# Running the first weight tiles behind each norm on unnormalised rows, in a two-layer hybrid encoder on one NeuronCore

## Chip, core and metric

The kernel runs on one of the NeuronCores of a Trainium2 chip. The metric is the device time of one execution in microseconds. Its time is 1211.0 us, the median of three runs (1208.95 to 1211.0).

## What is computed

Two layers run over 288 tokens (256 of a prompt, 32 of a later chunk), held with features on the partitions, so that one token is one column. Of the reference only this matters here:

```python
def rms_norm(x, g):
    xf = x.astype(jnp.float32)
    y = xf * lax.rsqrt(jnp.mean(xf * xf, axis=-1, keepdims=True) + EPS)
    return (y * g.astype(jnp.float32)).astype(x.dtype)
...
    h = rms_norm(x, g1) * (1 + scale1) + shift1
    y, rows = token_mixers(h, w_in, f_bias, lnv_g, lnv_b, w_s, b_s, w_branch, w_gate, b_gate, w_out, past)
    x = x + gate1 * y
    h = rms_norm(x, g2) * (1 + scale2) + shift2
    f, conv_state = conv_ffn(h, w_up, w_conv, b_conv, w_down, conv_prefix)
    x = x + gate2 * f
```

Scale, shift and gate come from c (adaLN), one set for the prompt and one for the later chunk. The root of a norm is one number per token. So a product W h equals the product of W with the unnormalised rows (x g (1 + scale)), times that number for each column, plus W shift. A last RMSNorm follows the second layer.

## The kernel before, in words

Every weight matrix is cut into pieces of 128 x 1024 floats, each the weights of one output tile of 128 features, or a third of one in the down projection. 142 pieces of a layer go through a ring of four slots. SP loads a piece into `raw`; ACT rounds it to the high part `whi` (L1052, L1059); POOL subtracts, which gives the low part `wlo` (L512); PE multiplies. ACT works three pieces ahead of PE (`AHEAD`). Rows are split the same way into `hh` and `hl`. PE forms high x high, high x low and low x high (L603, L604, L605), so a full tile of eight k steps takes 24 matmuls of 288 or 290 columns. The semaphores `hi_ready`, `lo_ready` and `piece_done` count pieces.

The order on each engine is written out by hand. A layer runs 26 input tiles, 32 gate and 8 branch pieces between which the four mixers are placed, 8 output tiles, 44 up tiles (with a convolution of width 3 on VectorE and ScalarE) and 24 down pieces. Around a norm all of it is serial. DVE adds each finished output or down tile into `x` (L1747, L1814). ACT squares it (L1070). `sums` on PE adds the eight squares over the partitions with a matrix of ones, eight fp32 matmuls at L574, all after the last tile. ACT takes logarithm and exponential (L1074, L1075). Three Newton steps on DVE follow (L1364 to L1366). Then for each of eight k DVE multiplies `x` by the root (L1428) and applies scale and shift (L1433), ACT makes `hh` (L1082), POOL makes `hl` (L530), and PE's first tile takes the k steps as they come.

At the start PE works on the modulation of layer 0 (quads, L556) while its 8 MB of weights arrive. The sums of `x` stand before the seventh quad. DVE takes the quads' rows (L1371), PE turns them (L565), DVE adds the bias (L1378) and forms the scale (L1385, L1386), and only then does the norm. In the first mixer tiles PE swaps rows for the rotary (`swap`, L646) and DVE rotates (L1446 to L1448).

In these rows `ps` is PSUM (8 banks). Input and output tiles alternate between banks 0 and 1, up tiles between 0 and 3, the sums are in bank 7.

## Time and profile before

| | |
|---|---|
| Median of 3 runs | 1211.0 us |
| The profiled execution: its time, its span | 1210.8 us, 1209.0 us |
| PE busy | 1138.7 us (94%), 8368 matmul records |
| PEld, DVE, ACT, POOL busy | 1028.3, 491.3, 572.6, 703.4 us |
| HBM traffic | 178 GB/s over the span |
| Share of the chain that ended last | PE 88%, DVE 7% |

### The profile page before, as it was taken

To read this page: it belongs to the slowest core of one execution; us is meant where nothing else is said; L and a number is where in the kernel's file an instruction comes from. 1 tells how busy PE (TensorE), PEld (TensorE's weight loads), DVE (VectorE), ACT (ScalarE), POOL (GpSimd) and SP (SyncE) were. 2 spreads that over 40 slices of the span, in tenths; PEclk is the share of its full clock that TensorE was granted. 3 is DMA by queue.
4 is the path that set the end of the run, shared out by engine and by line. 5 is a ranking of instruction groups with operands and counts; after the bars stand their busy time and mean duration, and the time that the engine had idled before them with its cause. 6 is when DMAs were issued, how large, how long until landed. Compare 5 with 4: busy or idle time off the path is not lost.

```text
span 1209.0 us, 22886 instructions
## 1 busy us (share of the span) xinstructions
PE 1138.7 (94%) x8368; PEld 1028.3 (85%) x8368; DVE 491.3 (41%) x1141; ACT 572.6 (47%) x1014; POOL 703.4 (58%) x320
## 2 busy tenths in 40 slices
PE   5699999999999899999969999999999979999997
PEld 1497888888889799999958788888889969999996
DVE  0535523446223644441043482345641354544202
ACT  1354444445444456554324635455544446556432
POOL 0664534545456677778846544344556657777882
PEclk9699999999999799999988999999999979999999
DMA  9655536755554244445554564575534414544551
GB/s 362 240 177 217 217 141 239 257 223 196 197 187 140 71 173 163 152 170 174 177 182 144 174 232 184 210 272 173 163 117 126 153 67 162 173 150 162 175 180 71
DMA packets 61814, 215.90 MB, mean 179 GB/s; under 512 B 7896, under 2 KB 8480, under 8 KB 61488
## 3 DMA queue, kind: packets, MB, share of 16 engines
q1 hardware_dynamic: 61744, 214.92, 51.0%
q8 instruction: 49, 0.80, 0.3%
q14 instruction: 21, 0.17, 0.0%
HBM read 209.85 MB, written 5.05 MB: 178 GB/s over the span
## 4 chain that ended last, share of the span: by engine, by line
PE 88%; DVE 7%; ACT 1%; DMA 1%; issue 1%; SPq 1%; POOL 0%; DVEq 0%; ACTq 0%
PE ps L603 25%; PE ps L604 24%; PE ps L605 24%; PE ps L556 4%; PE ps L574 1%; DVE work L1428 1%; DMA first<-mod_first 1%; DVE hup L1433 1%; PE ps L550 1%; DVE work L1433 1%; DVE ps L1573 1%; PE ps L770 1%; DVE merged L1581 1%; PE ps L736 1%; PE ps L646 1%
## 5 line engine op out<-in xcount | busy, mean ns | idle before, releaser
L512 POOL TENSOR_TENSOR wlo<-raw,whi 128x1024 fp32r<-128x1024 f32 x284 | 678.6, 2392 | 450.6 <-ACT whi L1052 383.7
L603 PE MATMUL ps<-hh,whi 128*128 128x288 f32 (+1 forms) x1760 | 541.9, 308 | 39.4 <-POOL hl L530 37.6
L604 PE MATMUL ps<-hl,whi 128*128 128x288 f32 (+1 forms) x1760 | 528.0, 300 | 0.0
L605 PE MATMUL ps<-hh,wlo 128*128 128x288 f32 (+1 forms) x1760 | 527.3, 300 | 0.0
L603 PEld LDWEIGHTS ps<-hh,whi 128*128 128x128 f32 x1760 | 337.6, 192 | 86.6 <-issue 65.4
L604 PEld LDWEIGHTS ps<-hl,whi 128*128 128x128 f32 x1760 | 339.7, 193 | 0.2
L605 PEld LDWEIGHTS ps<-hh,wlo 128*128 128x128 f32 x1760 | 338.3, 192 | 0.0
L1052 ACT ACTIVATE whi<-raw 128x1024 fp32r<-128x1024 f32 x204 | 214.3, 1053 | 125.8 <-PE ps L605 112.9
L1306 ACT ACTIVATE conv<-ps,vec 128x290 f32<-128x290 f32 x88 | 52.3, 595 | 114.7 <-DVE ps L1768 114.4
L604 PE MATMUL ps<-fal,whi 128*128 128x290 f32 x352 | 104.5, 297 | 0.0
L603 PE MATMUL ps<-fah,whi 128*128 128x290 f32 x352 | 104.3, 296 | 0.0
L605 PE MATMUL ps<-fah,wlo 128*128 128x290 f32 x352 | 104.2, 296 | 0.0
L1097 ACT ACTIVATE gb<-ps,vec 128x288 f32<-128x288 f32 x64 | 32.1, 502 | 118.0 <-PE ps L605 118.0
L1059 ACT ACTIVATE whi<-raw 128x1024 fp32r<-128x1024 f32 x80 | 85.1, 1064 | 0.0
L1088 ACT ACTIVATE proj<-ps,cst 128x288 f32<-128x288 f32 x52 | 26.1, 502 | 115.0 <-PE ps L605 114.9
L1770 DVE SCALAR_TENSOR_TENSOR conv<-ps,vec,conv 128x290 f32<-128x290 f32 x88 | 45.8, 520 | 84.4 <-ACT tail L1310 84.4
L604 PEld LDWEIGHTS ps<-fal,whi 128*128 128x128 f32 x352 | 66.8, 190 | 0.0
L605 PEld LDWEIGHTS ps<-fah,wlo 128*128 128x128 f32 x352 | 66.6, 189 | 0.0
L603 PEld LDWEIGHTS ps<-fah,whi 128*128 128x128 f32 x352 | 66.4, 189 | 0.0
L1814 DVE SCALAR_TENSOR_TENSOR x<-ps,mod,x 128x256 f32 (+1 forms) x32 | 10.3, 363 | 124.6 <-PE ps L605 124.6
L1771 DVE SCALAR_TENSOR_TENSOR conv<-ps,vec,conv 128x290 f32<-128x290 f32 x88 | 45.8, 520 | 11.9 <-DVE conv L1770 0.5
L603 PE MATMUL ps<-oh,whi 128*128 128x288 f32 x128 | 40.8, 319 | 6.8 <-DVE hl L1559 3.6
(216 smaller groups left out, 1138.1 us busy)
## 6 DMA issues: line engine op xcount, KB each, us to landing
raw<-stream SPq DMA_DIRECT2D x284, 512.0 KB, 4.3
mraw<-stream SPq DMA_DIRECT2D x40, 1024.0 KB
first<-mod_first SPq DMA_DIRECT2D x16, 512.0 KB, 10.7
o_proj<-proj SPq DMA_DIRECT2D x12, 288.0 KB
kvk<-keys_t SPq DMA_DIRECT2D x6, 512.0 KB, 3.8
kvv<-vals SPq DMA_DIRECT2D x6, 512.0 KB, 4.7
cst<-consts SPq DMA_DIRECT2D x1, 1238.0 KB, 17.5
x<-x_fm SPq DMA_DIRECT2D x1, 1152.0 KB, 11.7
```

What stands on the lines that cost most here:

```text
L512: nc.gpsimd.tensor_tensor(wlo[:, slot, :], raw[:, slot, :], whi[:, slot, :].bitcast(F32), ALU.subtract).then_inc(lo_ready, 1)
L556: i = mm(ps[32 * g:32 * g + 32, bank, :], cpad[:, at + 30 - 2 * j:at + 62 - 2 * j], pieces[g // 2][:, (g % 2) * 512:(g % 2 + 1) * 512], st ...
L603: mm(out, whi[:, slot, a:b], high, start=(i == 0 and wcols[2]), stop=False)
L604: mm(out, whi[:, slot, a:b], low, start=False, stop=False)
L605: last = mm(out, wlo[:, slot, a:b], high, start=False, stop=(i == n - 1 and wcols[3]))
L1052: A(whi[:, slot, :], raw[:, slot, :], ACT.Copy).then_inc(hi_ready, 1)
L1059: A(whi[:, slot, :], raw[:, slot, :], ACT.Copy).then_inc(hi_ready, 1)
L1088: A(proj[:, t, :], ps[:, bank, 0:T], ACT.Copy, scale=cst[:, C_QS + t:C_QS + t + 1]).then_inc(bank_free[bank], 1)
L1097: A(gb[:, g % GB, :], ps[:, t % 2, 0:T], ACT.Sigmoid if g in DIRECT else ACT.Identity, bias=vec[:, v:v + 1]).then_inc(bank_free[t % 2], 1)
L1306: A(conv[:, u, :], ps[:, UPB + u, 2:2 + CC], ACT.Identity, scale=vec[:, at(V_CONV + 2 * 2 * FT + g * FT)], bias=vec[:, at(V_CB + g * FT)])
L1770: conv_link(V.scalar_tensor_tensor(conv[:, u, :], up[:, 1:1 + CC], w[1], conv[:, u, :], ALU.mult, ALU.add))
L1771: V.scalar_tensor_tensor(conv[:, u, :], up[:, 0:CC], w[0], conv[:, u, :], ALU.mult, ALU.add).then_inc(convolved, 1)
```

## The change

At the first norm of layer 1 the first six input tiles (`NI`), and at the second norm of each layer the first four up tiles (`NU`), take unnormalised rows.

- While output or down tiles run, DVE adds a tile back in its PSUM bank (`add_back`). ACT squares it there and makes its scaled high part `oh`, DVE the low part `ol`. Then DVE copies it to `x` and frees the bank. Two extra columns of `oh` and `ol` carry the shift, so its product comes out in two extra columns of the tile.
- PE takes the sum of a tile's squares after the next tile (`sum_square`), the last one in the middle of the first unnormalised tile (`first_tile`).
- DVE multiplies a finished unnormalised tile by the root per column (`scale_tile`), ACT adds the shift's product (`take_scaled`, `shift_up`). In between, for the tiles behind, the rows are normalised in chunks (`normed`, `IN_CHUNKS`, `UP_CHUNKS`). The root stands in PSUM bank 7 and the product x * root in PSUM too. POOL takes lows of rows and of weights in order of arrival.
- The first three pieces of layer 1 are loaded and split before layer 0 ends.
- At the start the sums stand before the sixth quad. DVE takes root and x * root before the modulation and makes the weight lows of pieces 0 and 1. PE runs input tiles 0 and 1 together, k step by k step, and DVE makes `hl`, which POOL made before.
- SWAP_BANK, the turning of w and its spreading move by a bank or a tile. The loops over output and down tiles are written out.

The core of the diff:

```diff
+IN_CHUNKS = ((0, 1), (1, 3), (3, 5), (5, 7), (7, 8), (8, 8))
+UP_CHUNKS = ((0, 2), (2, 5), (5, 8))
...
+NI, NU = 6, 4
...
+                if l == 0:
+                    pool.wait_ge(hl_ready, upto(l, hl_ready, KT))
+                    q = Q_IN + 2
+                else:
+                    q = lows_and_norm(Q_IN + AHEAD, 1, ((3, 0, 1), (1, 1, 4), (1, 4, KT)))
+                lows(q, Q_UP + AHEAD)
+                q = lows_and_norm(Q_UP + AHEAD, 2, ((1, 0, 2), (1, 2, 5), (1, 5, KT)))
+                lows(q, NSPLIT + (AHEAD if l + 1 < DEPTH else 0))
...
+                def first_tile(out, slot, n):
+
+                    product(out, slot, (1, 0, True, False), u_terms[0:4], ul_ready, (n - 2) * KT)
+                    sum_square(l, n, KT - 1)
+                    return product(out, slot, (1, 0, False, True), u_terms[4:KT], ul_ready, (n - 2) * KT + 4)
...
+                for m in range(KT):
+                    t = OUT_TILE + m
+                    tile_piece(slot_for(l, Q_OUT + m), Q_OUT + m, t % 2, t // 2, merged_l if m == 0 else None)
+                    if m:
+                        sum_square(l, 2, m - 1)
...
+                    up_piece(slot_for(l, Q_UP + j), Q_UP + 4 + j, UPB + j, j + 1 if j >= 2 else None, hl_ready if j == 0 else None)
...
+                    for g, ((a, b), c, o) in enumerate(zip(((0, TP), (TP, T)), cols, (0, TP + 2))):
+                        i = A(oh[:, m, o:o + b - a], ps[:, bank, c:c + b - a], ACT.Copy, scale=norm_a[:, n - 1, m, g:g + 1])
+                    i.then_inc(uh_ready, 1)
...
                         q = Q_UP + 2 * p + g + AHEAD
-                        if q < NSPLIT:
-                            high(q, q % RING)
+                        if q >= Q_UP + AHEAD + 3:
+                            high(q)
...
+            dve.wait_ge(rstd_guess, upto(0, rstd_guess, 1))
+            newton(first_link, DM)
+            for k in range(KT):
+                V.tensor_tensor(work[:, k, :], x[:, k, :], rstd[:], ALU.mult).then_inc(x_scaled, 1)
+            mod_take(0, MOD_A_PAIRS)
+            for q in range(2):
+                dve.wait_ge(hi_ready, upto(0, hi_ready, q + 1))
+                V.tensor_tensor(wlo[:, q, :], raw[:, q, :], whi[:, q, :].bitcast(F32), ALU.subtract).then_inc(lo_ready, 1)
...
+                def normed(n, a, b):
+
+                    half = [ps[:, bank, 2:2 + T] for bank in (6, 2 if n == 1 else 1)]
+                    at = (n - 1) * KT
+                    for k in range(a, b + 1):
+                        if k < b:
+                            if k > 1:
+                                dve.wait_ge(h_scaled, upto(l, h_scaled, at + k - 1))
+                            V.tensor_tensor(half[k % 2], x[:, k, :], ps[:, 7, 0:T], ALU.mult).then_inc(x_scaled, 1)
+                        if k > a:
+                            dve.wait_ge(x_scaled, upto(l, x_scaled, at + k))
+                            affine(n, k - 1, half[(k - 1) % 2])
...
+                def add_back(n, m, bank, gate_at, cols):
+
+                    parts = list(enumerate(zip(((0, TP), (TP, T)), cols, (0, TP + 2))))
+                    for g, ((a, b), c, o) in parts:
+                        y = ps[:, bank, c:c + b - a]
+                        i = V.scalar_tensor_tensor(y, y, mod[:, gate_at + m, g:g + 1], x[:, m, a:b], ALU.mult, ALU.add)
+                    i.then_inc(residual, 1)
+                    dve.wait_ge(uh_ready, upto(l, uh_ready, (2 - n) * KT + m + 1))
+                    if m == 0:
+                        V.tensor_tensor(ol[:, :, TP:TP + 2], mod[:, 24 * (n - 1):24 * (n - 1) + KT, :],
+                                        oh[:, :, TP:TP + 2].bitcast(F32), ALU.subtract)
+                    for g, ((a, b), c, o) in parts:
+                        i = V.scalar_tensor_tensor(ol[:, m, o:o + b - a], ps[:, bank, c:c + b - a], norm_a[:, n - 1, m, g:g + 1],
+                                                   oh[:, m, o:o + b - a].bitcast(F32), ALU.mult, ALU.subtract)
+                    i.then_inc(ul_ready, 1)
+                    for g, ((a, b), c, o) in parts:
+                        i = V.tensor_copy(x[:, m, a:b], ps[:, bank, c:c + b - a])
+                    i.then_inc(bank_free[bank], 1)
...
+                convolve(0, 0, 0)
+                scale_tile(Q_UP + 3, up_bank(3), 2, None)
+                convolve(0, 0, 1)
```

Three places show how instructions move. The first is ACT behind the second norm of layer 0, where `whi<-raw` rounds a weight piece, `hh` is the high part of a row tile and `conv` a tile of the convolution. Before:

```order
L1323 ACT_TABLE_LOAD
L1052 ACTIVATE whi<-raw 128x1024 [waits raw_loaded1,ol_ready,piece_done,tail_stored,proj_stored]
L1306 ACTIVATE conv<-ps,vec 128x290 [waits state_in]
L1310 ACTIVATE tail<-ps 128x4
L1052 ACTIVATE whi<-raw 128x1024 [waits piece_done,raw_loaded2]
L1306 ACTIVATE conv<-ps,vec 128x290 [waits state_in]
L1310 ACTIVATE tail<-ps 128x4
L1052 ACTIVATE whi<-raw 128x1024 [waits piece_done,raw_loaded3]
L1306 ACTIVATE conv<-ps,vec 128x290 [waits state_in]
L1310 ACTIVATE tail<-ps 128x4
L1316 ACTIVATE ps<-conv 128x290 [waits convolved]
L1052 ACTIVATE whi<-raw 128x1024 [waits piece_done,raw_loaded0]
```

Now, from the last three high parts on:

```order
L1156 ACTIVATE hh<-hup 128x290 [waits h_scaled] x3
L1423 ACTIVATE conv<-ps,vec 128x290 [waits ol_ready,state_in,tail_stored,proj_stored]
L1427 ACTIVATE tail<-ps 128x4
L1384 ACTIVATE ps<-ps,shifts 128x256 [waits up_scaled]
L1384 ACTIVATE ps<-ps,shifts 128x32
L1423 ACTIVATE conv<-ps,vec 128x290 [waits state_in]
L1427 ACTIVATE tail<-ps 128x4
L1423 ACTIVATE conv<-ps,vec 128x290 [waits state_in]
L1427 ACTIVATE tail<-ps 128x4
L1433 ACTIVATE ps<-conv 128x290 [waits convolved]
L1109 ACTIVATE whi<-raw 128x1024 [waits piece_done,raw_loaded0]
L1423 ACTIVATE conv<-ps,vec 128x290 [waits state_in]
```

Before, a piece was rounded ahead of every convolved tile; now the first one after the norm's three (into slot 0, the seventh up piece) stands behind three convolved tiles.

The second is POOL at the same norm. Before:

```order
L512 TENSOR_TENSOR wlo<-raw,whi 128x1024 [waits hi_ready]
L511 REGISTER_ALU
L512 TENSOR_TENSOR wlo<-raw,whi 128x1024 [waits hi_ready]
L519 REGISTER_ALU
L519 COMPARE_AND_BRANCH
L512 TENSOR_TENSOR wlo<-raw,whi 128x1024 [waits hi_ready] x2
L530 TENSOR_TENSOR hl<-hup,hh 128x290 [waits hh_ready] x8
L519 UNCONDITIONAL_BRANCH
```

Now:

```order
L542 REGISTER_ALU
L542 COMPARE_AND_BRANCH
L535 TENSOR_TENSOR wlo<-raw,whi 128x1024 [waits hi_ready] x4
L553 TENSOR_TENSOR hl<-hup,hh 128x290 [waits hh_ready] x2
L535 TENSOR_TENSOR wlo<-raw,whi 128x1024 [waits hi_ready]
L553 TENSOR_TENSOR hl<-hup,hh 128x290 [waits hh_ready] x3
L535 TENSOR_TENSOR wlo<-raw,whi 128x1024 [waits hi_ready]
L553 TENSOR_TENSOR hl<-hup,hh 128x290 [waits hh_ready] x3
```

The eight lows of rows stood together; now a weight low goes ahead of each chunk of two, three and three.

The third is DVE at the start, up to the first k steps. Before:

```order
L1371 COPY mod_rows<-ps 128x512 [waits mod_read,c_ready]
L1378 TENSOR_TENSOR mod<-ps,mvec 128x4x2 [waits rows_turned]
L1378 TENSOR_TENSOR mod<-ps,mvec 128x4x2 x3
L1385 TENSOR_SCALAR norm_a<-mod 128x16 [waits mod_ready]
L1386 TENSOR_TENSOR norm_a<-norm_a,mvec 128x16 [waits c_ready]
L1364 SCALAR_TENSOR_TENSOR rstd<-ps,rstd 128x288 [waits rstd_guess,c_ready]
L1365 SCALAR_TENSOR_TENSOR rstd<-rstd 128x288 [waits dve_own]
L1366 SCALAR_TENSOR_TENSOR rstd<-rstd 128x288 [waits dve_own]
L1428 TENSOR_TENSOR work<-x,rstd 128x288 [waits dve_own]
```

Now:

```order
L1490 SCALAR_TENSOR_TENSOR ps<-ps,rstd 128x288 [waits rstd_guess,c_ready]
L1491 SCALAR_TENSOR_TENSOR ps<-ps,rstd 128x288 [waits c_ready]
L1492 SCALAR_TENSOR_TENSOR rstd<-ps,rstd 128x288 [waits c_ready]
L1532 TENSOR_TENSOR work<-x,rstd 128x288 [waits c_ready]
L1532 TENSOR_TENSOR work<-x,rstd 128x288 x7
L1497 COPY mod_rows<-ps 128x512 [waits mod_read]
L1536 TENSOR_TENSOR wlo<-raw,whi 128x1024 [waits hi_ready] x2
L1504 TENSOR_TENSOR mod<-ps,mvec 128x4x2 [waits rows_turned]
L1504 TENSOR_TENSOR mod<-ps,mvec 128x4x2 x3
L1511 TENSOR_SCALAR norm_a<-mod 128x16 [waits mod_ready]
L1512 TENSOR_TENSOR norm_a<-norm_a,mvec 128x16 [waits c_ready]
L1554 TENSOR_SCALAR work<-work,norm_a,mod 128x256 [waits x_scaled,c_ready]
```

The root and the eight products of x moved ahead of the taking of the modulation's rows (`mod_rows`), and two weight lows (`wlo`) stand behind it.

## Rows read from the trace of the kernel before

**Rows 1.** Stretches; each pair: busy us (count) of PE, PEld, DVE, ACT, POOL; clock, DMA, GB/s

```profile
57.00:387.00 330.00, 326.04 (x2518) 281.08 (x2517) 140.16 (x311) 156.71 (x267) 171.47 (x73) 0.99 0.57 202
387.00:410.00 23.00, 15.87 (x65) 12.58 (x64) 13.63 (x34) 8.91 (x16) 10.17 (x11) 0.70 0.10 38
410.00:616.00 206.00, 206.00 (x1539) 206.00 (x1538) 72.77 (x187) 106.72 (x200) 152.69 (x64) 1.00 0.50 169
616.00:645.00 29.00, 15.81 (x64) 12.55 (x63) 18.20 (x29) 11.47 (x18) 17.04 (x13) 0.65 0.38 124
645.00:967.00 322.00, 316.55 (x2449) 277.92 (x2448) 136.56 (x304) 156.50 (x267) 172.46 (x73) 1.00 0.53 182
```

**Rows 2.** Waits of the whole span: engine, line, releaser, us in total, times, longest

```profile
PEld ps L603 <- issue: 69.0, 56, 12.2
...
PE ps L603 <- POOL hl L530: 37.6, 26, 11.8
```

**Rows 3.** Timeline of PE at the start: start us, us, engine, line, operation [idle before]

```profile
25.03 6.14 PE L574 MATMUL ps<-work,cst 128*128 128x288 f32 x16
31.10 1.92 PE L556 MATMUL ps<-first,cpad 128*32 128x512 f32 x16
...
43.93 0.58 PE L603 MATMUL ps<-hh,whi 128*128 128x288 f32 x1 [8.96 <-POOL hl L530]
```

**Rows 4.** Timeline of ACT at the start

```profile
32.15 2.93 ACT L1052 ACTIVATE whi<-raw 128x1024 fp32r<-128x1024 f32 x3
...
61.41 0.50 ACT L1088 ACTIVATE proj<-ps,cst 128x288 f32<-128x288 f32 x1 [1.76 <-PE ps L605]
```

**Rows 5.** Timeline of DVE at the start

```profile
33.16 0.69 DVE L1371 COPY mod_rows<-ps 128x512 f32<-128x512 f32 x1 [14.28 <-PE ps L556]
...
41.07 0.83 DVE L1428 TENSOR_TENSOR work<-x,rstd 128x288 f32<-128x288 f32 x2
41.81 0.62 DVE L1433 TENSOR_SCALAR work<-work,norm_a,mod 128x256 f32<-128x256 f32 x2
...
42.71 1.10 DVE L1433 TENSOR_SCALAR work<-work,norm_a,mod 128x256 f32<-128x256 f32 x2
```

**Rows 6.** Timeline of PE at the second norm of layer 0

```profile
387.48 4.05 PE L574 MATMUL ps<-work,cst 128*128 128x288 f32 x16
396.91 0.58 PE L603 MATMUL ps<-hh,whi 128*128 128x290 f32 x1 [5.38 <-POOL hl L530]
```

**Rows 7.** Timeline of DVE before, in and after the second norm of layer 0

```profile
371.69 0.65 DVE L1747 SCALAR_TENSOR_TENSOR x<-ps,mod,x 128x256 f32<-128x256 f32 x2 [2.54 <-PE ps L605]
...
387.69 0.64 DVE L1747 SCALAR_TENSOR_TENSOR x<-ps,mod,x 128x256 f32<-128x256 f32 x2 [2.57 <-PE ps L605]
...
392.57 0.46 DVE L1364 SCALAR_TENSOR_TENSOR rstd<-ps,rstd 128x288 f32<-128x288 f32 x1 [3.98 <-ACT rstd L1075]
...
426.98 0.16 DVE L1768 COPY ps<-vec 128x2 f32 x1 [0.43 <-PE ps L605]
428.12 0.52 DVE L1770 SCALAR_TENSOR_TENSOR conv<-ps,vec,conv 128x290 f32<-128x290 f32 x1 [0.98 <-ACT tail L1310]
```

**Rows 8.** Timeline of POOL beside it: a weight low and an activation low

```profile
369.70 2.40 POOL L512 TENSOR_TENSOR wlo<-raw,whi 128x1024 fp32r<-128x1024 f32 x1 [0.40 <-ACT whi L1052]
...
395.97 0.80 POOL L530 TENSOR_TENSOR hl<-hup,hh 128x290 fp32r<-128x290 f32 x1 [7.92 <-ACT hh L1082]
```

**Rows 9.** Stretch of 1 us in which PE's clock came back at the start, columns as in Rows 1

```profile
56.00:57.00 1.00, 1.00 (x8) 1.00 (x7) 0.00 (x0) 0.00 (x0) 1.00 (x1) 0.80 0.66 180
```

**Rows 10.** Timeline of PE at the first norm of layer 1

```profile
616.52 4.05 PE L574 MATMUL ps<-work,cst 128*128 128x288 f32 x16
```

**Rows 11.** Timeline of ACT behind it: input tile 4 is read out of its bank

```profile
655.58 0.50 ACT L1088 ACTIVATE proj<-ps,cst 128x288 f32<-128x288 f32 x1 [1.73 <-PE ps L605]
```

**Rows 12.** Timeline of DVE in the rotation behind it

```profile
657.73 2.08 DVE L1447 TENSOR_TENSOR scr<-proj,cst 128x288 f32<-128x288 f32 x1
```

**Rows 13.** Waits of PE from 645 to 967 us

```profile
PE ps L603 <- DVE hl L1559: 2.2, 2, 1.8
```

433 lines of the change are left out of this document (269 added, 164 removed).

## The prediction

> **What bounds the kernel now.** I read first the table of stretches [rows 1], to see where PE is not full. In the long stretches it is: 326.0 of 330 us in layer 0's mixer, 206.0 of 206 in its up and down tiles, at clock 1.00. In the 23 us around the second norm it is busy 15.9 us at 0.70, in the 29 us around layer 1's first norm 15.8 us at 0.65. The page shows layer 1's second norm like layer 0's. The waits say who holds PE [rows 2]: the low parts of rows, 37.6 us in 26 waits, and 69.0 us in which the weight load had only its turn to wait for, most of it ahead of those. So the bound is PE, and time is to be had only at the start, at three norms and at the end. A matmul costs 206 / 1539 = 0.134 us, a tile of 24 costs 3.2 us. Everything else has slack: a weight low takes POOL 2.4 us of those 3.2 [rows 8].
>
> Then I read each norm on the timelines. Behind layer 0's output tiles PE starts eight sums at 387.48 that take 4.05 us, and starts its first up tile at 396.91, after 5.4 us idle [rows 6]. The idle time is root, Newton steps and first k. After it each k step comes at DVE's pace, about 1.4 us: 0.3 for a product beyond the overlap and 1.10 for the affine pair [rows 5]. At layer 1's first norm the sums start at 616.52 and are as long [rows 10]; there, three weight lows on POOL also stand in DVE's way.
>
> **What one k costs DVE.** Its 32-column operation should end 0.2 us after the 256-column one. The pair took 0.62 us while POOL was idle and 1.10 us once POOL made lows [rows 5]. The adding into x, which reads PSUM, x and a scalar, took 0.65 us beside a running weight low and 0.64 us beside the end of one [rows 7, 8]. So what reads PSUM isn't held. In the change x * root and the affine go through PSUM at the three later norms. I take 0.95 us a k: 0.37 for the product (0.83 us for two overlapped ones [rows 5]) and 0.58 for the pair. The bounds are 0.9 and, if PSUM operands were held after all, today's 1.4.
>
> This is where the Trainium skill bears on it. Its page "SBUF — State Buffer", section "Who interferes with whom", says that a VectorE instruction with two SBUF inputs, or in a two-port mode, takes turns with a GpSimd instruction that reads SBUF. By that rule the eight k of a norm take 7.6 us; by today's pace they take 11.2, and the sum would be 7 us poorer over the two second norms.
>
> **Second norm, two times.** Time 0 is the end of the last output tile. *Removed from the wait:* six of eight sums (0.49 us each, 2.9 us) run earlier between tiles. They are PE's work as before, so I subtract them. *Up tiles 0 to 3* need no root: sum 6, four k, sum 7 end at 2.6. Sum 7's square is there by then (add 0.64, square 0.5). The tiles end at 13.8 without a stall. *The root:* logarithm and exponential to 3.7, both by ACT's 0.50 us for 288 columns [rows 11], three steps of 0.46 and a little [rows 7] to 5.2. *DVE then:* scale tile 0 (0.6) and copy the root (0.45) to 6.2, eight k (7.6) and two scalings (1.2) to 15.1. *POOL:* three weight lows (7.2) and eight row lows of 0.80 (6.4) [rows 8]; it starts at 2.8, waits about 2.9 for the first high part, ends at 19.3. So tile 4, which may begin at 13.8, gets its last k at 19.3 and ends at 19.9, and tile 5 ends at 23.1. *What is late next:* the sixth piece's successor. Its rounding stands on ACT behind three convolved tiles. These begin at 15.1, for DVE was busy: 2.3 us for each (copy at 426.98, first multiply at 428.12, two of 0.52 [rows 7]) plus scaling and shifting tile 3 (1.2). ACT's part of the third ends at 21.6, silu and rounding at 23.0, POOL's low at 25.4. Tile 6 runs from 25.6 to 28.8, and DVE takes it up at 29.0. Before, DVE took it up at 426.98 [rows 7], which is 39.5 after 387.48. Gain 39.5 - 29.0 - 2.9 = 7.6. From then on DVE and ACT need under 3.2 us a tile, and no bank is missed.
>
> Costs ahead of it: one small operation of `add_back` at tile 0 reads two SBUF operands and will stand behind a weight low, up to 2.4 us. A bank now comes free 3.3 us after its tile (add 0.64, ACT's rounding 1.0 and square and high part 1.1, low 0.6, copy 0.5), and PE wants it after 4.2 us (sum, tile, sum). So nothing at seven tiles and 0.5 us at the first. Then the clock: PE idles 1.9 us within tile 4 and 2.5 us ahead of tile 6. In the trace 1.8 us idle [rows 13] left the clock at 1.00 [rows 1], and 5.4 us [rows 6] lost it. I charge 0.6 us; the bounds are 0 and 3.2, one tile more for a stretch at half speed. **Gain 6.5 each, 13 in all**, bounds 3 to 10 each.
>
> **First norm of layer 1.** Six tiles without the root last from 0 to 20.4 with the two sums. DVE: root by 5.6, then six scalings (0.6), the copy and eight k end near 20; ACT empties each bank before PE wants it again, the tightest being tile 0's at 7.1 to 7.6. POOL: five weight lows and eight row lows, 18 us from 3.1 on, end at 21.5, before PE reaches the eighth k of tile 6. No stall there, and the clock stays. Tile 4 is read out at 17.3 instead of 655.58 - 616.52 = 39.1 [rows 10, 11]. Minus 2.9: 18.9. The loads of layer 1's vectors, keys and values go as before after the first pieces; two extra pieces ahead of them delay none that is wanted within 10 us. New: DVE rotates late, at 21, among POOL's lows. Its two-SBUF-operand step took 2.08 us instead of 0.45 beside one [rows 12], and PE's third swap waits for the first rotation: 1.5 us, bounds 0 and 3. **Gain 17.4.**
>
> **Start.** Sums begin at 22.5 instead of 25.03 [rows 3], still partly at 1.2 GHz, and end at 28.8. The last quads end at 31.7, by their loads (31.10 + 1.92 before). DVE: root known at 29.8, Newton to 31.3, eight products of 0.38 to 34.4, taking the rows 0.7 [rows 5], two weight lows (estimate 1.1 each by the 0.45 us of 288 columns), turning hidden beside them, scale ready at 38.2. First `hl` at 39.9, then one k per 1.0 us (affine pair 0.62, low 0.4): last at 46.8. PE needs 6 x 0.24 us a k cold for the two tiles, so it is full from 39.9, recovers its clock near 44, after some 4 us of full work (before, it came back between 56 and 57, once no k was waited for [rows 9]) and ends both at 48.4. Tile 2 waits for its low, which POOL begins at 46.9: 49.35, read out at 52.75 instead of 61.41 [rows 4]. The roundings, 2.93 us for three [rows 4], move no later than they are needed. **Gain 8.7**, bounds 6 and 10.
>
> **End.** The last two sums wait for the last square: ready at 2.25 after the last tile plus 2.9 moved ahead, against 4.05: **loss 1.1.** Moving the turning of w by a tile and writing loops out cost nothing: PE has the same matmuls.
>
> **Sum.** 8.7 + 17.4 + 13.0 - 1.1 = 38.0 us less than the profiled execution's 1210.8, that is 1172.8; the median is 0.2 higher, so **1173**.
>
> **The rivals.**
> *The late split decides.* At the second norms tile 6 comes later than 25.6, PE falls to 1.2 GHz and climbs back twice, and at the start it stays at 1.2 GHz through both joined tiles (8 x 1.45 = 11.6 from 39.9). For it: once lost, the clock stayed away long enough to average 0.70 over 23 us [rows 1], though PE had begun again at 396.91 [rows 6]. Against: gaps are half of today's. Gain 3.7 at each second norm, 6 at the start: 1173 + 5.6 + 2.7 = 1181. Chance 0.23.
> *More than that.* Handshakes overlap better, tile 6 is ready when tile 5 ends, and the rotation isn't held: 3 us more at each second norm, 1.5 at the first, 1 at the start: 1164.5. Chance 0.14.
> *VectorE stands behind GpSimd all the time, and the kernel is slower.* If DVE's operations with one SBUF operand were held too, each output tile's add and low would wait for a weight low. A bank would be free after 5.7 us at the least where the tile period is 3.7: 16 tiles x 2.0 = 32 us. The 24 k would each wait 0.8 us for a row low, 19 us. Together 51 against a gain of 38: 1224. It decides from a hold of some 3 us a tile. Against it stand the 0.65 and 0.64 us [rows 7] beside POOL's lows [rows 8]. Chance 0.03.
> *It doesn't happen.* If PE waited for the root all the same (through a bank that isn't free), the time would stay at 1211. The order shows up tiles waiting for unnormalised rows alone. Chance 0.02.
>
> **How the numbers follow.** My case has 0.58. The range reaches over the two neighbours, a little beyond their values for the bounds of single terms: 1163 to 1186. It leaves out the last two rivals and tails, about 0.15. A measurement tells 0.2% (2.4 us) from no change; faster 0.95, same 0.02, slower 0.03.
>
> **What would show it.** In the new profile: no idle PE between the last down tile and the seventh input tile of layer 1, clock 1.00 there. At the second norms two gaps, within up tile 4 for row lows on POOL, and before tile 6 for a weight low released by a late rounding on ACT. DVE's affine pairs at 0.6 us beside POOL. First matmul at 40 us. Wrong would be: matmuls of output tiles waiting for banks, gaps over 5 us behind the fourth up tile, or a PE that waits within the first six input tiles.

## The result and the profile after

The changed kernel takes 1175.0 us, the median of four runs (1171.43 to 1177.0), against 1210.9 for the kernel before on the same chip: a ratio of 0.9704, 95% interval 0.9677 to 0.9731. In a later group it came to 1173.2 (five runs, 1171.6 to 1174.1; 0.9684, 0.9670 to 0.9697). Forecast were 1173 and a range of 1163 to 1186. The profiled execution is the fastest run, 1171.43 us with a span of 1169.7; before, the span was 1209.0. So what is read from this trace adds up to 39.3 us, and the medians differ by 35.9 and, in the later group, by 38.1.

The stretches of [rows 1], cut at the new places of the three norms. Each pair is busy us (count) of PE, PEld, DVE, ACT, POOL; then clock, DMA share, GB/s:

```profile
50.00:382.00 332.00, 326.48 (x2508) 280.35 (x2507) 149.38 (x342) 159.09 (x280) 173.61 (x73) 0.99 0.57 204
382.00:411.00 29.00, 24.87 (x176) 23.72 (x176) 20.90 (x67) 19.75 (x44) 19.43 (x15) 1.00 0.25 86
411.00:604.00 193.00, 193.00 (x1428) 192.27 (x1427) 74.04 (x200) 106.94 (x209) 148.47 (x63) 1.00 0.50 173
604.00:633.00 29.00, 27.91 (x199) 26.85 (x199) 22.41 (x62) 17.65 (x35) 23.93 (x17) 1.00 0.64 239
633.00:936.00 303.00, 297.52 (x2302) 258.96 (x2302) 138.30 (x325) 151.35 (x270) 158.66 (x67) 1.00 0.51 180
936.00:964.00 28.00, 25.35 (x169) 24.20 (x168) 20.43 (x67) 18.49 (x41) 18.43 (x14) 0.94 0.29 99
```

In 29 us around a norm PE now makes 199 and 176 matmuls at clock 1.00, where it made 64 in 29 and 65 in 23 at 0.65 and 0.70 [rows 1]. Outside the norms PE is as full as before, but for a wait of 1.6 us at layer 0's output tiles that is shown below. The waits for row lows, 37.6 us in [rows 2], have shrunk to the second and third of these rows, 6.9 us; the first is for weight lows, the last for a bank (columns as there):

```profile
PE ps L637 <- POOL wlo L535: 3.6, 3, 2.2
PE ps L637 <- DVE hl L1607: 3.5, 1, 3.5
PE ps L637 <- POOL hl L553: 3.4, 2, 1.7
PE ps L637 <- DVE x L1601: 1.6, 1, 1.6
```

A read-out is ScalarE's copy of a finished tile out of its bank. Setting the same read-outs of the two traces side by side gives the account. The third input tile is read out at 50.92 instead of 61.41 [rows 4]: 10.5 us at the start. From one stage to the next this shift grows by 5.6 us at layer 0's second norm, 16.9 at layer 1's first, 7.9 at its second, and shrinks by 1.5 at the end: 39.4, and the spans differ by 39.3. As an example, one gate tile behind layer 1's first norm, before and now, 32.9 us apart:

```profile
763.38 0.50 ACT L1097 ACTIVATE gb<-ps,vec 128x288 f32<-128x288 f32 x1 [0.99 <-PE ps L605]
```

```profile
730.49 0.50 ACT L1192 ACTIVATE gb<-ps,vec 128x288 f32<-128x288 f32 x1 [0.99 <-PE ps L639]
```

The start, PE's timeline and ACT's (start us, us, engine, line, operation [idle before]), the places of [rows 3, 4]:

```profile
22.57 5.12 PE L606 MATMUL ps<-work,cst 128*128 128x288 f32 x16
27.62 2.78 PE L590 MATMUL ps<-first,cpad 128*32 128x512 f32 x24
...
38.77 0.58 PE L637 MATMUL ps<-hh,whi 128*128 128x288 f32 x1 [3.47 <-DVE hl L1607]
...
39.38 0.45 PE L639 MATMUL ps<-hh,wlo 128*128 128x288 f32 x1
...
41.72 0.30 PE L637 MATMUL ps<-hh,whi 128*128 128x288 f32 x1
...
47.39 0.41 PE L637 MATMUL ps<-hh,whi 128*128 128x288 f32 x1 [0.71 <-POOL wlo L535]
```

```profile
50.92 0.50 ACT L1183 ACTIVATE proj<-ps,cst 128x288 f32<-128x288 f32 x1 [1.81 <-PE ps L639]
```

The duration of a matmul falls from 0.45 to 0.30 at 41.7: the granted clock is 0.50 in 39 to 41 us and 1.00 in 42 to 47, so PE is back at 2.4 GHz some 3 us behind its first product matmul.

Layer 0's second norm. The last output tile ends at 381.96. VectorE's row work, ScalarE's late rounding, GpSimd behind it, and PE's two gaps (the place of [rows 6 to 8]):

```profile
388.98 1.43 DVE L1554 TENSOR_SCALAR hup<-ps,norm_a,mod 128x256 f32<-128x256 f32 x4
...
390.82 0.81 DVE L1566 TENSOR_TENSOR ps<-x,ps 128x288 f32<-128x288 f32 x2
```

```profile
403.82 1.06 ACT L1109 ACTIVATE whi<-raw 128x1024 fp32r<-128x1024 f32 x1
```

```profile
404.95 4.72 POOL L535 TENSOR_TENSOR wlo<-raw,whi 128x1024 fp32r<-128x1024 f32 x2 [3.73 <-ACT whi L1109]
```

```profile
399.73 0.40 PE L637 MATMUL ps<-hh,whi 128*128 128x290 f32 x1 [1.72 <-POOL hl L553]
...
407.36 0.40 PE L637 MATMUL ps<-hh,whi 128*128 128x290 f32 x1 [2.20 <-POOL wlo L535]
```

Up tile 6 starts 25.4 us behind the last output tile. In layer 1 it is 25.4 as well (936.92 to 962.35), though PE ran at half clock from 956.2 to 959.4 there: the tile before was longer and the gap shorter (0.72 us). That fall cost nothing.

Layer 1's first norm, the place of [rows 10 to 12]. No wait in the first six tiles, then:

```profile
624.02 1.06 ACT L1109 ACTIVATE whi<-raw 128x1024 fp32r<-128x1024 f32 x1 [3.46 <-DMA raw<-stream]
```

```profile
626.56 0.37 PE L637 MATMUL ps<-hh,whi 128*128 128x288 f32 x1 [1.09 <-issue]
```

And a wait that was not forecast, at layer 0's output tiles: a VectorE product of 16 columns with both operands in SBUF is held, that is, it doesn't end until GpSimd's weight low beside it does, and the third output tile waits for the bank. The product unheld (0.17 us) and held:

```profile
353.86 0.17 DVE L1512 TENSOR_TENSOR norm_a<-norm_a,mvec 128x16 f32<-128x16 f32 x1
...
354.28 2.39 DVE L1512 TENSOR_TENSOR norm_a<-norm_a,mvec 128x16 f32<-128x16 f32 x1
```

In the kernel before, the same product was held as well, 2.28 us, and no tile waited for a bank behind it:

```profile
364.70 2.28 DVE L1386 TENSOR_TENSOR norm_a<-norm_a,mvec 128x16 f32<-128x16 f32 x1
```

In the changed kernel, GpSimd's weight low beside it, and the third output tile:

```profile
354.24 4.81 POOL L535 TENSOR_TENSOR wlo<-raw,whi 128x1024 fp32r<-128x1024 f32 x2 [6.11 <-ACT whi L1109]
```

```profile
360.21 0.37 PE L637 MATMUL ps<-hh,whi 128*128 128x288 f32 x1 [1.58 <-DVE x L1601]
```

### The profile page after: what moved, and what is told of

Its sections match the earlier page's. It is cut to its first block, busy times and chain, and to the rows that moved or that the text cites. A ratio compares the mean times of both kernels' runs of the same rounds, so it can differ in the third digit from the quotient of the medians.

```text
span 1169.7 us, 22931 instructions
## 1 busy us (share of the span) xinstructions
PE 1119.6 (96%) x8368; PEld 1017.8 (87%) x8368; DVE 515.3 (44%) x1297; ACT 591.3 (51%) x1095; POOL 691.8 (59%) x310
## 4 chain that ended last, share of the span: by engine, by line
PE 86%; DVE 6%; POOL 2%; issue 2%; ACT 2%; DMA 1%; SPq 1%; DVEq 0%; POOLq 0%; ACTq 0%
PE ps L637 25%; PE ps L638 23%; PE ps L639 23%; PE ps L590 4%; PE ps L606 2%; POOL wlo L535 1%; PE ps L584 1%; DMA first<-mod_first 1%; POOL hl L553 1%; DVE ps L1758 1%; PE ps L798 1%; DVE merged L1766 1%; PE ps L764 1%; PE ps L674 1%; PE ps L754 1%
## 5 line engine op out<-in xcount | busy, mean ns | idle before, releaser
L637 PE MATMUL ps<-hh,whi 128*128 128x288 f32 (+1 forms) x1648 | 501.4, 304 | 15.2 <-POOL wlo L535 3.6
L638 PE MATMUL ps<-hl,whi 128*128 128x288 f32 (+1 forms) x1648 | 489.6, 297 | 0.0
L639 PE MATMUL ps<-hh,wlo 128*128 128x288 f32 (+1 forms) x1648 | 489.0, 297 | 0.0
L637 PEld LDWEIGHTS ps<-hh,whi 128*128 128x128 f32 x1648 | 312.3, 190 | 55.9 <-issue 37.7
L638 PEld LDWEIGHTS ps<-hl,whi 128*128 128x128 f32 x1648 | 313.1, 190 | 0.6
L639 PEld LDWEIGHTS ps<-hh,wlo 128*128 128x128 f32 x1648 | 312.1, 189 | 0.0
L1961 DVE SCALAR_TENSOR_TENSOR conv<-ps,vec,conv 128x290 f32<-128x290 f32 x88 | 45.7, 520 | 85.8 <-ACT tail L1427 85.8
L637 PE MATMUL ps<-oh,whi 128*128 128x288 f32 (+1 forms) x240 | 75.8, 316 | 6.8 <-DVE hl L1744 3.7
L639 PE MATMUL ps<-oh,wlo 128*128 128x288 f32 (+1 forms) x240 | 71.6, 298 | 0.0
L638 PE MATMUL ps<-ol,whi 128*128 128x288 f32 (+1 forms) x240 | 71.4, 297 | 0.0
## 6 DMA issues: line engine op xcount, KB each, us to landing
cst<-consts SPq DMA_DIRECT2D x1, 1238.0 KB, 17.3
x<-x_fm SPq DMA_DIRECT2D x1, 1152.0 KB, 11.8
```

Source lines behind the costliest of these rows:

```text
L637: mm(out, whi[:, slot, a:b], high, start=(i == 0 and wcols[2]), stop=False)
L638: mm(out, whi[:, slot, a:b], low, start=False, stop=False)
L639: last = mm(out, wlo[:, slot, a:b], high, start=False, stop=(i == n - 1 and wcols[3]))
L1961: conv_link(V.scalar_tensor_tensor(conv[:, u, :], up[:, 1:1 + CC], w[1], conv[:, u, :], ALU.mult, ALU.add))
```

## The experiments

Every run carries the whole change but for its edit. So that a few tenths can be read, each trace was cut at five marks: the read-out of the third input tile (M0), and the first Newton step of the four later norms (layer 0's second, layer 1's first and second, the last). A median is of five runs; the changed kernel's own row is of four. The runs were made in several groups, in each of which the kernel before came to 1210.9 to 1211.3 us.

```
run                     M0    to 2nd norm   to 1st norm   to 2nd norm  to last   median
                              layer 0       layer 1       layer 1      norm      us
changed kernel          50.9  334.8         222.0         333.0        221.4     1175.0
a_again                 52.2  336.4         222.0         332.5        221.4     1173.2
e_wait                  51.8  334.9         223.3         336.6        222.7     1177.9
e_sbuf                  51.7  334.8         226.4         335.6        227.3     1184.6
e_round                 51.7  334.8         221.1         332.4        220.5     1172.0
e_loads                 52.1  336.3         222.0         332.3        221.5     1174.0
e_scale                 52.1  332.6         222.1         332.6        221.4     1172.0
e_pool_low              50.9  334.8         222.1         334.9        221.3     1173.4
e_block                 51.4  334.9         226.4         343.4        224.5     1185.0
e_turn                  50.7  336.3         222.1         334.8        221.4     1174.6
e_best                  50.4  332.7         221.1         335.9        219.9     1168.7
e_best2                 49.6  332.6         221.1         332.6        219.8     1165.5
e_few                   51.5  332.9         221.0         332.4        219.9     1167.2
```

**The changed kernel again.** 

> The changed kernel as it is, as the run that the others of this group are read against, and to see why its times lay between 1171.4 and 1177.0 us. Theory: the spread comes from loads that land late, since the rounding of the ninth weight piece of layer 1 waited 3.46 us for its raw transfer even in the fastest run, and ScalarE's order puts the fifth input tile's read-out behind it. Then a slower run shows longer waits for raw transfers at the same clock. Rival: the spread is the granted clock (0.983 to 0.988 in these runs; 0.005 of 1170 us is 5.9 us at most), and then the slower run shows the same waits and a stretch at the lower clock somewhere.

Its profiled execution has a span of 1172.0, 2.3 us more, and the wait for the load was shorter there (2.91 us), so my theory of the spread falls, and its rival, the granted clock, is what the two traces show. The difference is 1.3 us at the start and 1.5 between M0 and the second norm. At the start the sums begin within 0.1 us of each other and take 6.25 us instead of 5.12, with a mean clock of 0.60 in 23 to 28 us instead of 0.84:

```profile
22.68 6.25 PE L606 MATMUL ps<-work,cst 128*128 128x288 f32 x16
```

Later, one and the same stall at the third output tile (1.57 us) was followed by a fall of the clock, which in the first trace it was not. The stretch of 8 us around it, first of the changed kernel, then of this run:

```profile
358.00:366.00 8.00, 6.42 (x44) 5.89 (x45) 4.25 (x14) 4.16 (x10) 4.53 (x3) 1.00 0.70 254
```

```profile
358.00:366.00 8.00, 6.27 (x32) 5.60 (x31) 3.93 (x15) 2.85 (x7) 4.70 (x2) 0.79 0.57 190
```

**A wait for PE that should cost nothing at the second norms.**

```diff
                         i.then_inc(piece_done, 1)
+                        if t == 2:
+                            pe.wait_ge(h_scaled, upto(l, h_scaled, 5))
...
                     i.then_inc(piece_done, 1)
+                    if j == 2:
+                        pe.wait_ge(h_scaled, upto(l, h_scaled, KT + 6))
```

> TensorE waits, ahead of the fourth unnormalised tile, for a normalised row that it doesn't use: the sixth one at both second norms (ready some 2.5 us later than that tile now starts), the fifth one at the first norm of layer 1 (2.7 us later). Theory: at the second norms the seventh tile's start is set by the row work and the weight low behind it (25.4 us behind the last out tile), and TensorE has 1.7 and 2.2 us of waiting there to give, so both cost 0 to 0.5; at the first norm of layer 1 the tiles are in TensorE's own time and the wait costs 1.6 to 2.7 (the 1.1 us of idle before the seventh tile may take some). Sum +1.6 to +3.5 us. Rival, TensorE-bound at all three: +7.7 us. Rival, row-bound at all three: 0.

PE was held 3.29 us at each second norm and 2.81 at the first norm of layer 1:

```profile
396.97 0.40 PE L637 MATMUL ps<-oh,whi 128*128 128x290 f32 x1 [3.29 <-DVE hup L1558]
409.52 0.41 PE L637 MATMUL ps<-hh,whi 128*128 128x290 f32 x1 [1.09 <-POOL wlo L535]
619.78 0.57 PE L637 MATMUL ps<-oh,whi 128*128 128x290 f32 x1 [2.81 <-DVE work L1558]
```

The cost by marks is 1.3 us at either second norm, and 3.6 to 4.1 at the first norm, where the clock averaged 0.89 in 615 to 630 us after it had been 1.00; the median rose by 4.7. So the first norm hides nothing and pays the clock on top, and of the 3.3 us at a second norm 1.3 show. My 0 to 0.5 was too low, and the trace names the reason. ScalarE's rounding, for which tile 6's weight low waits, stands behind the scaling and shifting of the fourth tile, and the fourth tile was what I delayed: the rounding moved from 403.82 to 405.95 while Newton began 0.9 later, 1.2 us net. VectorE now waits 1.15 us for that tile:

```profile
402.03 0.16 DVE L1581 COPY shifts<-ps 128x2 f32<-128x2 f32 x1 [1.15 <-PE ps L639]
```

```profile
395.00:405.00 10.00, 8.03 (x48) 8.03 (x49) 6.56 (x23) 4.15 (x12) 7.07 (x8) 0.83 0.29 105
```

But the delay alone doesn't make this wait. The clock fell behind the gap, and 14 matmuls of the fourth tile, from 398.05 to 401.42, started 0.24 us apart instead of 0.134, which is 1.5 us. By this estimate, at full clock the tile would have been done at 400.5, before VectorE was free for it at 400.9. So the row work hides the 3.3 us, and the price is that of the fall. In layer 1 it is the same (a wait of 1.14 us, clock 0.83 in 955 to 965).

**The root from SBUF.**

```diff
-                            V.tensor_tensor(half[k % 2], x[:, k, :], ps[:, 7, 0:T], ALU.mult)
+                            V.tensor_tensor(half[k % 2], x[:, k, :], rstd[:], ALU.mult)
```

> The products of the rows by the root take the root from SBUF and not from the bank, as before the change, all else alike; eight products at each of three norms. Theory: with both operands in SBUF a product that runs beside one of GpSimd's lows is held until that ends, 1.5 to 2.4 us where 0.45 is its own; some 5 of 8 are hit at a norm. The second norms are bound by the row work and pay all of it, 4 to 9 us each; the first norm of layer 1 has slack and pays 0 to 3. Sum +8 to +18 us. Rival: the choice of operand is nothing, 0 us within 1.

The median rose by 11.5 us, in the marks 4.4 and 5.9 at the second norms and 2.6 to 3.1 in the stretch that holds the first. Of the last, 1.1 to 1.6 come at the norm itself and the rest from a fall of the clock at layer 1's output tiles (0.91 in 905 to 925 us). VectorE's timeline at layer 0's second norm shows a pair of products of its own length, then pairs and single ones held beside GpSimd:

```profile
388.98 0.83 DVE L1566 TENSOR_TENSOR ps<-x,rstd 128x288 f32<-128x288 f32 x2
...
391.57 1.61 DVE L1566 TENSOR_TENSOR ps<-x,rstd 128x288 f32<-128x288 f32 x2
...
393.88 1.87 DVE L1566 TENSOR_TENSOR ps<-x,rstd 128x288 f32<-128x288 f32 x1
```

In layer 0 VectorE is through with the rows 16.5 us behind its first Newton step instead of 12.1, and these 4.4 us are the whole loss. In layer 1 up tile 6 is 4.3 us late in the same way, and a fall of the clock behind the gap ahead of it (3.46 us; 0.89 in 970 to 985 us) brings the rest. GpSimd pays a little too, 2.61 us for a weight low between these rows where it took 2.42 at the same place. So some 9 of the 13 us gained at the two second norms hang on one copy of the root into a bank, and 10 with that fall.

**The tenth up piece rounded early.**

```diff
                     if r is None and p == 0:
+                        high(Q_UP + 6)
                         shift_up(3)
...
-                    if r is None:
-                        q = Q_UP + 2 * p + g + AHEAD
-                        if q >= Q_UP + AHEAD + 3:
-                            high(q)
-                    else:
+                    if r is not None:
```

> ScalarE rounds the tenth up piece (the one whose weight low the seventh up tile waits for) ahead of the fourth tile's shift, and not behind the second pair's first convolution; nothing else is moved. Theory: GpSimd sits idle 3.7 us for that rounding, so its weight low begins right behind the row lows and the gap before the seventh tile (2.2 us in layer 0, 0.7 in layer 1) closes: -2 to -3.5 us. Rival: the row lows are what is late, or the convolution that ScalarE does later holds the bank of another tile and the gap comes back there: 0 within 1.

By marks -0.9 and -1.0, by median -1.2, half of what I expected. GpSimd's low now begins at 401.95, right behind the row lows, and the gap ahead of tile 6 is gone. Half of it comes back one tile later:

```profile
410.35 0.40 PE L637 MATMUL ps<-hh,whi 128*128 128x290 f32 x1 [1.20 <-POOL wlo L535]
```

The next rounding is in the loop and as late as before.

**Loads ahead of the vectors.**

```diff
-                for q in range(RING if l == 0 else 2 * RING):
+                for q in range(RING if l == 0 else 2 * RING + 2):
...
-                    if l == 0 or q >= 2 * RING:
+                    if l == 0 or q >= 2 * RING + 2:
```

> In layer 1 the ninth and tenth weight pieces are requested ahead of the layer's vectors, the spatial weights and the keys, not behind them. Theory: the rounding of the ninth piece waited 2.9 and 3.5 us for its transfer, and ScalarE read the fifth input tile out behind it, so that TensorE stood 0.5 to 1.1 us ahead of the seventh input tile; this wait goes: -0.5 to -1.1 us. Rival: the vectors are now what is late, and VectorE's rotations behind the sixth input tile wait for them and hold the banks: 0 to +2 us.

The wait for the load and PE's idle time before the seventh input tile are gone from the trace. The stretch behind this norm is 332.3 us against 332.5 in the repeat. The median, 1174.0, is no better. The edit gives 0.2 us if anything: PE's 0.5 to 1.1 us of idle time there were mostly given back later.

**The scale of the second norm earlier.**

```diff
                        mod_add(MOD_BANK, upto(l, rows_turned, 1), MOD_A, MOD_B_PAIRS // 2, l * NMV + MOD_A)
+                        dve.wait_ge(mod_ready, upto(l, mod_ready, 1))
+                        norm_scale(in_order, 1, 4 * KT, slice(l * NMV + M_G2, l * NMV + M_G2 + KT))
...
-                norm_scale(in_order, 1, 4 * KT, slice(l * NMV + M_G2, l * NMV + M_G2 + KT))
```

> The second norm's scale of every row (two small VectorE operations per layer) is made in the mixer, right behind the modulation it needs, and not directly ahead of the first out tile. Theory: there the 128x16 product, whose operands both lie in SBUF, was held 2.39 us by GpSimd's weight low in layer 0 of the changed kernel, the first residual add came late and TensorE stood 1.6 us for the bank at the third out tile; in layer 1 no low ran there and nothing waited. -1.3 to -1.8 us, all in layer 0. Rival: the first out tile's own low on VectorE (its shift columns, both operands in SBUF) is what is held, and the wait stays: 0 within 0.5.

The stretch to the second norm shrank to 332.6, by 2.2 us against the changed kernel's trace and 3.8 against the repeat's, where the clock had fallen. The stall is gone from PE's timeline. By the median it is -1.2; the profiled execution's own start was 1.2 later than the changed kernel's (M0).

**The start's weight lows back on GpSimd, with the root in a bank.**

```diff
                 if l == 0:
+                    lows(Q_IN, Q_IN + 2)
...
             newton(first_link, DM)
+            first_link(V.tensor_copy(ps[:, 7, 0:T], rstd[:]))
             for k in range(KT):
-                V.tensor_tensor(work[:, k, :], x[:, k, :], rstd[:], ALU.mult).then_inc(x_scaled, 1)
+                V.tensor_tensor(work[:, k, :], x[:, k, :], ps[:, 7, 0:T], ALU.mult).then_inc(x_scaled, 1)
             mod_take(0, MOD_A_PAIRS)
-            for q in range(2):
-                dve.wait_ge(hi_ready, upto(0, hi_ready, q + 1))
-                V.tensor_tensor(wlo[:, q, :], raw[:, q, :], whi[:, q, :].bitcast(F32), ALU.subtract).then_inc(lo_ready, 1)
```

> At the start GpSimd makes the lows of the first two weight pieces again, and VectorE copies the root into the bank and takes it from there for its eight products, so that none of them has two operands in SBUF beside GpSimd. Theory: VectorE's two weight lows (2.35 us for both) stood in the chain that sets TensorE's first matmul; GpSimd makes them from 30.5 to 35.3 us, under the products, and the first matmul comes 1.5 to 2.3 us earlier (the copy costs 0.45). -1.5 to -2.3 us. Rival: the copies of the modulation rows and VectorE's row work are held by GpSimd all the same, and the two weight lows cost at least what they gave: 0 to +3 us. This is the part of the change that moved these lows to VectorE, undone in a form that avoids what it was moved for.

Nothing was gained: from the first Newton step to the first row low VectorE needs 9.1 us, and 9.3 with the two weight lows. They had stood in the time in which PE turned the modulation rows:

```profile
34.02 0.68 DVE L1498 COPY mod_rows<-ps 128x512 f32<-128x512 f32 x1
36.27 0.38 DVE L1505 TENSOR_TENSOR mod<-ps,mvec 128x8 f32<-128x8 f32 x4 [1.58 <-PE ps L600]
```

So with the root in a bank the place of these two lows neither costs nor gives anything. Whether they would hold VectorE's products on GpSimd with the root in SBUF, which is what they were moved for, was not run.

**And the rows copied ahead of the products.** `mod_take(0, MOD_A_PAIRS)` now stands ahead of the eight products, all else as in the run before. 

> The run before that gave GpSimd the first two weight lows came out 0.2 us faster within its noise, since VectorE then stood 1.6 us for TensorE's turn of the modulation rows. Here the copy of the rows goes ahead of the eight products as well, so that TensorE turns them under the products; the weight lows stay with GpSimd. Theory: VectorE's chain from the first Newton step to the first row low was 9.3 us with its two weight lows and 9.1 without them; it is now 3 links, the copy of the root, the rows' copy, eight products, the modulation, the scale and the first row: 1.5 + 0.5 + 0.7 + 3.0 + 0.4 + 0.4 + 1.0, some 7.3 us. -1.8 to -2.2 us. Rival: GpSimd's lows (to 35.5 us) now lie beside the scale's two-SBUF product, which is held, or TensorE waits for the second weight low: -1 us or nothing.

The chain is 7.5 us long (29.78 to 37.26), 1.8 less, as computed. Of it 1.2 us arrive at the third tile's read-out (20.9 us from the first Newton step against 22.0 to 22.1): PE now stands 4.28 us before its first product matmul, instead of 3.47, and though both kernels take that matmul at half clock, the full clock is back 5.3 us behind it and not 3 (at 43.2 against 41.7). The median did not fall, 1174.6. The rest of the trace says why: 1.5 us more in layer 0 with a fall of the clock, as in the repeat, and in layer 1 a stall of 1.78 us at the third output tile, which the changed kernel and its repeat do not have.

**The order of arrival undone.**

```diff
-IN_CHUNKS = ((0, 1), (1, 3), (3, 5), (5, 7), (7, 8), (8, 8))
-UP_CHUNKS = ((0, 2), (2, 5), (5, 8))
+IN_CHUNKS = ((0, 8),) + 5 * ((8, 8),)
+UP_CHUNKS = ((0, 8), (8, 8), (8, 8))
...
-                    q = lows_and_norm(Q_IN + AHEAD, 1, ((3, 0, 1), (1, 1, 4), (1, 4, KT)))
+                    q = lows_and_norm(Q_IN + AHEAD, 1, ((3, 0, KT), (1, KT, KT), (1, KT, KT)))
...
-                q = lows_and_norm(Q_UP + AHEAD, 2, ((1, 0, 2), (1, 2, 5), (1, 5, KT)))
+                q = lows_and_norm(Q_UP + AHEAD, 2, ((1, 0, KT), (1, KT, KT), (1, KT, KT)))
```

> The order of arrival is undone at the three norms that have unnormalised tiles: behind the first of these, all eight rows are scaled, rounded and split in one piece, and only then do the other tiles' scaling and the weight lows follow. Theory: at the first norm of layer 1 two banks carry the tiles, so the second tile's read-out comes at 619.8 and not at 613.8, and the fourth tile waits 5 us for its bank: +5 to +7 us with the fall of the clock. At the second norms every unnormalised tile has a bank of its own, VectorE's and GpSimd's work sum up to the same, and the seventh tile starts as before: 0 to +1.5 us each. Sum +5 to +9 us. Rival, that the order is worth nothing: 0 within 1; rival, that it is worth the same at all three norms: +15 us or more.

The median rose by 11.8 us against the repeat, more than the 5 to 9 I expected. At layer 1's first norm PE stood 6.23 us for the second tile's read-out:

```profile
625.86 0.58 PE L637 MATMUL ps<-oh,whi 128*128 128x290 f32 x1 [6.23 <-ACT proj L1162]
```

With the low clock behind it (0.83 in 626 to 636 us) the tiles there come some 7 us late, the upper end of what I allowed. The rest of the 10.9 us in that stretch lies at the output tiles of layer 1: the clock falls behind the 1.83 us gap ahead of the first of them (0.85 in 920 to 930 us), and the third stalls for 1.58 us, at full clock. At the thirteenth up tile the second norms are 2.9 us late each, more than the 1.5 I allowed (the 4.4 of the table has a stall of 1.1 us at the third down tile in it, by its releaser the same wait for a bank). In one block a row low comes every 1.16 us, each waiting 0.35 us for ScalarE, so GpSimd's next weight low begins at 399.24; PE's two gaps become one of 5.2 us, and the clock goes.

**Together, first try.** The edits of e_round, e_scale, e_loads and e_turn, and one at the end:

```diff
                     if m:
-                        sum_square(l + 1, 1, m - 1)
-            sum_square(DEPTH, 1, KT - 1)
+                        if m < KT - 2 or l + 1 < DEPTH:
+                            sum_square(l + 1, 1, m - 1)
+            for k in range(KT - 3, KT):
+                sum_square(DEPTH, 1, k)
```

> All that helped, together: the second norm's scale in the mixer, the tenth up piece rounded early, the start as in the run beside this one, the ninth and tenth weight loads ahead of the vectors, and in the last layer the sum of the sixth square behind the last down tile, into the 0.7 us in which TensorE waits there for the last square. Theory, from the marks of the runs: -2.2 (the stall and its fall of the clock), -1.9 (0.98 and 0.92 at the two second norms), -2.0, -0.4, -0.5: -7 us from 1173.2, so 1166 us. Rival: the parts share what they give (an earlier start or low only lengthens a wait for a load): 1169 to 1171 us.

1168.7 us, 2.7 more than the sum of the parts and just under the rival's 1169 to 1171. Every stretch is as short as its edit had made it (the last by 0.6 for the sums), except that between the norms of layer 1: 335.9 instead of 332.6. There the other two-SBUF operation of the output tiles, `add_back`'s low of the shift columns, was held by a weight low, and the third tile waited for its bank:

```profile
910.99 2.39 DVE L1592 TENSOR_TENSOR ol<-mod,oh 128x16 fp32r<-128x16 f32 x1 [1.34 <-ACT oh L1141]
```

```profile
908.63 7.14 POOL L535 TENSOR_TENSOR wlo<-raw,whi 128x1024 fp32r<-128x1024 f32 x3 [6.11 <-ACT whi L1112]
```

```profile
914.52 0.37 PE L638 MATMUL ps<-hh,whi 128*128 128x288 f32 x1 [1.85 <-DVE x L1599]
```

The same operation is held in e_turn (2.29 us). Which of the two is caught, and in which layer, changes from kernel to kernel with the phase between the engines, that is, with whether one of GpSimd's weight lows happens to run at that moment. This is read off the traces; no run set the phase.

**Together, the shifts through a bank.**

```diff
+                    shift = ps[:, 6, 496:496 + 2 * KT].rearrange("p (k g) -> p k g", g=2)
+                    if m == 0:
+                        in_order(V.tensor_copy(shift, mod[:, 24 * (n - 1):24 * (n - 1) + KT, :]))
                     dve.wait_ge(uh_ready, upto(l, uh_ready, (2 - n) * KT + m + 1))
                     if m == 0:
-                        V.tensor_tensor(ol[:, :, TP:TP + 2], mod[:, 24 * (n - 1):24 * (n - 1) + KT, :],
-                                        oh[:, :, TP:TP + 2].bitcast(F32), ALU.subtract)
+                        V.tensor_tensor(ol[:, :, TP:TP + 2], shift, oh[:, :, TP:TP + 2].bitcast(F32), ALU.subtract)
```

> As the combination before, and the first out tile's and first down tile's low of the shift columns takes the shifts from a bank, where VectorE has copied them, and not from SBUF. Theory: in the combination's layer 1 that 128x16 operation was held 2.39 us by a weight low, TensorE stood 1.85 us for the bank at the third out tile, and from the first Newton step of the first norm to that of the second it took 335.9 us against the 332.6 of the runs in which nothing was held there; so with no two-SBUF operation left at these places both layers take 332.6 whatever the phase, -3.2 us in layer 1: 1165 to 1166 us, and the runs lie closer together. Rival: what is held is any VectorE operation beside GpSimd's first low there, or the copy adds to the chain: 1168 to 1170 us.

1165.5 us (1165.0 to 1166.8), ratio to the kernel before 0.9631 (0.9618 to 0.9644). Both layers take 332.6. The two rows show the operation at its own length inside a weight low:

```profile
908.96 0.18 DVE L1595 TENSOR_TENSOR ol<-ps,oh 128x16 fp32r<-128x16 f32 x1 [1.34 <-ACT oh L1141]
```

```profile
906.24 4.75 POOL L535 TENSOR_TENSOR wlo<-raw,whi 128x1024 fp32r<-128x1024 f32 x2 [6.11 <-ACT whi L1112]
```

**Without the new start and loads.** As the run before, less the edits of e_turn and e_loads. 

> The same without the new start (GpSimd's first two weight lows, the rows' copy first) and without the earlier loads. Theory: the start gave 1.2 us from the first Newton step to the read-out of the third tile, and the loads 0.2 to 0.8, so this one is 1.4 to 2.0 us slower than the run beside it: 1167 us. Rival: both were inside the spread, and this one is the same within 0.5 us.

1167.2 us, 1.7 more. Of the 1.9 us between the two M0 (51.5 and 49.6), 0.7 stand ahead of the first Newton step, where neither edit acts: the sums begin 0.36 us later and take 5.49 us instead of 5.12. So the new start is worth 1.2 us once no phase-dependent stall hides it; the loads can't be told from nothing.

## Why the prediction was right, and where it was not

**The time** came out at 1175.0 and 1173.2 against 1173.0; term by term it was 8.7 + 6.5 + 17.4 + 6.5 - 1.1 forecast and 10.5 + 5.6 + 16.9 + 7.9 - 1.5 measured in the profiled execution, the fastest. The mechanism of each gain is as forecast; one cost had another cause and size, as told below. That the sum is so close is partly luck: the terms are off by +1.8, -0.9, -0.5, +1.4 and -0.4.

**PSUM operands are not held.** This carried the second norms. The affine pair took 1.43 us for two k, 0.7 where I took 0.58 each, the product 0.41 for my 0.37; VectorE was through 15.8 us behind the last output tile against 15.1. Had the root stayed in SBUF, the second norms would have lost 4.4 and 5.9 us, as e_sbuf shows (with a fall of the clock in the second figure); my figure for that case was 7 over both. The rule of the Trainium skill that I weighed ("SBUF — State Buffer", section "Who interferes with whom") agrees with e_sbuf, e_best and e_best2: two SBUF inputs beside a GpSimd instruction are held, one is not.

**The chain at a second norm** stood nearly as written: the last row low at 19.3 us (forecast 19.3), the late rounding done at 22.9 (23.0), tile 6 at 25.4 (25.6), with the two gaps at the places named, 1.7 and 2.2 us for 1.9 and 2.5. e_wait and e_round bear it out, the first with the addition that PE's fourth tile joins the chain when the clock falls within it. The 7.6 us before deductions became 7.8 (5.6 plus the 2.2 that e_scale returned) and 7.9. I had charged 0.6 for the clock, and it cost nothing there.

**The step that failed** is the 0.5 us for "one small operation of `add_back` at tile 0". The kind of cost was right, its place and size were not. In layer 0 the product that makes the scale, which I had passed over because it had stood there before at no cost, was held 2.39 us. Two output tiles later it was a PE gap of 1.6 us, worth 2.2 us and, with the clock, up to 3.8. In layer 1 it depends on the phase: nothing in the changed kernel, 2.3 to 3.3 us in e_turn, e_pool_low and e_best. I had also said that a bank is never missed beyond 0.5 us, and named waits of output tiles for banks as a sign of being wrong; this is that sign, once.

**Layer 1's first norm**: no PE wait in six tiles and clock 1.00, as forecast. Tile 6 starts at 22.6 us instead of about 20.4. "Two extra pieces ahead of them delay none that is wanted within 10 us" was wrong. The ninth piece waited 3.5 us behind vectors and keys, and the fifth tile was read out at 21.7 instead of 17.3. But e_loads shows that this costs the end next to nothing. The 1.5 us for the held rotation did not come: an operation was held 2.45 us, and PE did not wait for it. The two errors cancel within 0.5 us, which is luck.

**The start** gave 10.5 in the first trace and 9.2 in the repeat instead of 8.7. In the first the sums ended at 27.7, not 28.8; in the repeat they ended at 28.9, so this part is the clock's doing in one execution and no gain of the change. The clock was back at 41.7, not 44. The two weight lows that I put into the chain cost nothing (e_pool_low), since the turn of the rows stood in the same place; I had those two side by side and counted only one.

**The end** lost 1.5 for 1.1.

**The rivals.** A late split at half clock (1181) did not come: each gap stayed under 2.3 us, the stretch of layer 0 kept 1.00, and the one fall at layer 1's second norm (0.94 over the stretch) cost nothing. "More than that" (1164.5) wanted tile 6 ready as tile 5 ends; it was 2.2 and 0.7 us late. VectorE held all the time (1224) is excluded by the pairs beside GpSimd.

**What stays open** is why the same 1.6 us stall loses the clock in some executions and not in others, and whether the 1177.0 us run had one fall more. Only the profiled executions show where it falls; for the run of 1177.0 us there is its mean clock alone, 0.983 against 0.988 in the fastest. Other numbers of unnormalised tiles than six and four were not run either.
